# A fused encoder layer on one Trainium2 core: a deeper buffer ring in its first expert stage, a thinner spread of gate batches, and more expert visits in the sample's front

## The reference

```python
h = rmsnorm(x, norm1_g)
na_q, na_k, na_v, r_q, r_k, r_v, r_g = split(h @ w_in)
na_o = neighbourhood_attention(na_q, na_k, na_v, na_rpb)     # 8 heads of 64
ret_o = bidirectional_retention(r_q, r_k, r_v, r_g, ...)     # 4 heads of 128
x = x + concat([na_o, ret_o]) @ w_out
h = rmsnorm(x, norm2_g)
q = h @ w_q                                   # 8 heads, two halves of 128
s = einsum('thpd,hpnd->thpn', q, sub_keys)    # 128 keys for each half
# per head: top 16 of each half, top 16 of the 256 sums -> 16 experts and gates
a = gelu(einsum('td,tkd->tk', h, u[experts]))
x = x + einsum('tk,tkd->td', gates * a, v[experts])
y = rmsnorm(x, final_g)
```

## Time and profile before

| what | value |
|---|---|
| median of 3 runs | 2820.98 us (2814.81 to 2833.08) |
| profiled execution, its own time | 2804.88 us |
| its span | 2803.1 us |
| PE busy | 2431.6 us (87%) |
| DVE busy | 1768.2 us (63%) |
| POOL busy | 1256.0 us (45%) |
| ACT busy | 951.8 us (34%) |
| DMA | 613.60 MB, mean 219 GB/s |

### The profile page before, as it was taken

One profiled execution on the slowest core, in us unless ns is written; L12 is line 12 of the kernel. 1 busy time (PEld: TensorE's weight loads), 2 busy tenths in 40 slices (PEclk: granted clock), 3 DMA queues, 4 the chain that ended last, 5 costly groups with the idle time before them and its releaser, 6 DMA issues.

```text
span 2803.1 us, 34174 instructions
## 1 busy us (share of the span) xinstructions
PE 2431.6 (87%) x12633; PEld 2013.2 (72%) x12633; DVE 1768.2 (63%) x3403; ACT 951.8 (34%) x1426; POOL 1256.0 (45%) x932
## 2 busy tenths in 40 slices
PE   7969788788897898899999987978899798989897
PEld 6759777778875566688888776757677677777775
DVE  5564861132156668659885768768566577777776
ACT  4344344544322322333333322323222233333333
POOL 0001676423453342564444346473677465555530
PEclk9979999999998899899999999999999999999998
DMA  5424556546664443563444477695999899999994
GB/s 188 136 98 145 181 177 208 178 159 188 211 213 134 134 162 137 183 243 119 144 147 145 137 267 277 219 325 164 362 317 326 289 328 325 324 323 324 326 323 173
DMA packets 269189, 613.60 MB, mean 219 GB/s; under 512 B 35920, under 2 KB 134736, under 8 KB 268384
## 3 DMA queue, kind: packets, MB, share of 16 engines
q1 hardware_dynamic: 199008, 402.46, 42.5%
q0 software_dynamic: 67712, 201.61, 21.0%
q10 hardware_dynamic: 2304, 7.34, 0.7%
HBM read 529.51 MB, written 81.79 MB: 218 GB/s over the span
## 4 chain that ended last, share of the span: by engine, by line
PE 47%; DVE 18%; DMA 10%; POOL 9%; ACT 8%; issue 6%; SPq 2%; DVEq 0%; ACTq 0%
PE ps L784 35%; PE ps L814 9%; DMA raw<-in_experts 6%; POOL sp_lo L453 5%; DVE hot_a L1439 3%; DVE acc L1472 3%; ACT sp_hi L671 2%; DVE acc_odd L1472 2%; ACT v_hi L687 2%; DVE hot_b L1435 2%; POOL picked L457 2%; DMA picked<-in_experts,vidx 2%; POOL a_got L462 2%; DMA band<-in_band 1%; SPq L349 1%
## 5 line engine op out<-in xcount | busy, mean ns | idle before, releaser
L784 PE MATMUL ps<-ht_hi,sp_hi 128*128 128x256 f32 (+1 forms) x2048 | 719.0, 351 | 131.7 <-POOL sp_lo L453 73.8
L457 POOL DMA_INDIRECT picked<-in_experts,vidx x384 | 435.8, 1135 | 671.6 <-DVE acc L1472 363.0
L784 PE MATMUL ps<-ht_lo,sp_hi 128*128 128x256 f32 (+1 forms) x2048 | 697.1, 340 | 0.0
L784 PE MATMUL ps<-ht_hi,sp_lo 128*128 128x256 f32 (+1 forms) x2048 | 696.6, 340 | 0.0
L453 POOL TENSOR_TENSOR sp_lo<-raw,sp_hi 128x1024 fp32r<-128x1024 f32 x152 | 384.0, 2528 | 685.0 <-ACT sp_hi L671 685.0
L784 PEld LDWEIGHTS ps<-ht_hi,sp_hi 128*128 128x128 f32 x2048 | 394.8, 193 | 196.0 <-POOL sp_lo L453 91.9
L462 POOL DMA_INDIRECT a_got<-acts,aidx x384 | 432.9, 1127 | 118.4 <-issue 116.2
L784 PEld LDWEIGHTS ps<-ht_hi,sp_lo 128*128 128x128 f32 x2048 | 394.7, 193 | 42.2
L784 PEld LDWEIGHTS ps<-ht_lo,sp_hi 128*128 128x128 f32 x2048 | 395.4, 193 | 36.3
L784 PE MATMUL ps<-v_hi,w_hi 128*128 128x512 f32 x768 | 307.7, 401 | 64.7 <-DVE w_lo L1499 52.4
L679 ACT ACTIVATE act_g<-ps 128x256 f32<-128x256 f32 (+1 forms) x256 | 125.8, 491 | 657.5 <-PE ps L784 653.3
(11 more groups left out here) (180 smaller groups left out, 3440.0 us busy)
## 6 DMA issues: line engine op xcount, KB each, us to landing
raw<-in_experts SPq DMA_DIRECT2D x256, 512.0 KB, 3.6
v_raw<-in_experts SPq DMA_DIRECT2D x128, 512.0 KB, 5.0
raw<-in_front SPq DMA_DIRECT2D x104, 512.0 KB, 3.5
acts<-act_g SPq DMA_DIRECT2D x128, 256.0 KB, 3.3
gates<-stage SPq DMA_DIRECT2D x24, 1024.0 KB, 12.3
act_in<-acts SPq DMA_DIRECT2D x128, 192.0 KB, 5.1
g_in<-gates SPq DMA_DIRECT2D x128, 192.0 KB, 5.3
acts<-act_g SPq DMA_DIRECT2D x128, 128.0 KB, 3.5
```

Of the source, the lines that this page charges most:

```text
L457: pool.indirect_dma_start(picked[n % SLOTS][:, :], None, v_rows, bass.IndirectOffsetOnAxis(ap=vidx[:, n // P, n % P:n % P + 1], axis=0)).t ...
L784: last = pe.matmul(out, l, r, start=start and k == 0, stop=stop and k == 2, skip_group_check=True)
```

## The change

It has five parts.

- **Ring.** In the first u stage all four slots are used: `u_slot` is `step % RING`, each slot has its own semaphore (`u_landed`), loads and `sp_hi` run four steps ahead. POOL splits steps 0 to 55, DVE all of 56 to 127. The sample's first chunks are loaded in steps 124 to 127 and not in step 56, and their split follows the u stage. `EXP_AT` of tile 1 moves from step 42 to 46.
- **Gate batches.** Two to a row, over 16 rows for each tile, from 184, 209 and 234. PE does half of a row's matmuls after each batch. DVE builds them one step ahead, and splits row `step + 1` first. Visits are dealt out by weight, 11 to a step whose next row has gates, 8 to another.
- **Last tile on chip.** Tile 5's gates stay in `stage`; only 256 columns of gates are read back a row, and `w_f` becomes two multiplications, 128 columns from `stage` and 256 from `g_in`. For this `act_in`, `g_in`, `w_f`, `w_hi`, `w_lo`, `x2d`, `fgain`, `junk2` and `acc2` move; several lie where `ht_hi` was, so their first writes wait for the last scores (`a_done` = 256).
- **Visits.** 118 and not 93 in the sample's front: two and not one after each of 10 + 8 + 7 chunks. 138 are left for stage 4.
- **Slots of the front's chunks.** `slot_of` is `c % RING` for both sequences, and the first two loads of the second u stage wait for the last two chunks' split.

```diff
-GATES_AT = {SPARSE: 184, SPARSE + 1: 200, SPARSE + 2: 216}
-GATE_ROWS = 4
+GATES_AT = {SPARSE: 184, SPARSE + 1: 209, SPARSE + 2: 234}
+GATE_ROWS = 16
 TURN_AT = {SPARSE: 161, SPARSE + 1: 171, SPARSE + 2: 179}
-EXP_AT = {0: 25, 1: 42, 2: 140, 3: 152, 4: 164, 5: 174}
+EXP_AT = {0: 25, 1: 46, 2: 140, 3: 152, 4: 164, 5: 174}
...
-FRONT_VISITS = 93
+FRONT_VISITS = 118
...
         acc = [sb("acc0", V0, [P, D_MODEL]), sb("acc1", V0 + 4 * KB, [P, D_MODEL]),
-               sb("acc2", R0 + 28 * KB, [P, D_MODEL])]
+               sb("acc2", A0 + 24 * KB, [P, D_MODEL])]
...
-        act_in = sb("act_in", R0, [P, 2, HALF])
-        g_in = sb("g_in", R0 + 3 * KB, [P, 2, HALF])
-        w_f = sb("w_f", R0 + 6 * KB, [P, 2, HALF])
-        w_hi = sb("w_hi", R0 + 9 * KB, [P, 2, HALF], F32R)
-        w_lo = sb("w_lo", R0 + 12 * KB, [P, 2, HALF], F32R)
-        x2d = sb("x2d", R0 + 16 * KB, [P, SPARSE, D_MODEL])
-        fgain = sb("fgain", R0 + 32 * KB, [P, D_MODEL])
...
+        act_in = sb("act_in", A0 + 21 * KB, [P, 2, HALF])
+        g_in = sb("g_in", A0 + 52 * KB, [P, 2, 2 * P])
+        w_f = sb("w_f", 16 * KB, [P, 2, HALF])
+        w_hi = sb("w_hi", 19 * KB, [P, 2, HALF], F32R)
+        w_lo = sb("w_lo", 22 * KB, [P, 2, HALF], F32R)
+        x2d = sb("x2d", 25 * KB, [P, SPARSE, D_MODEL])
...
         def slot_of(q, c):
-            return (c + 2 * q) % RING
+            return c % RING
...
         for step in range(STEPS):
-            if step < 64 or step < N_KEYS and step % 2 == 0 or N_KEYS <= step < N_KEYS + 56:
+            if step < 56 or N_KEYS <= step < N_KEYS + 56:
                 by_pool[step] = len(by_pool) + 1
             else:
                 by_dve[step] = len(by_dve) + 1
...
-            return step % 2 + 2 * (step // N_KEYS)
+            return step % RING if step < N_KEYS else 2 + step % 2
+
+        def u_landed(step):
+
+            if step < N_KEYS:
+                return u_in[step % RING], 16 * (step // RING + 1)
+            return u_in[step % 2], 16 * (N_KEYS // RING + (step - N_KEYS) // 2 + 1)
...
             def load_chunk(q, c):
                 if c >= RING:
                     sp.wait_ge(*counted(q, "lo_ready", c - RING + 1))
-                elif q and c < 2:
-                    sp.wait_ge(*counted(0, "lo_ready", C_END))
                 elif q:
                     sp.wait_ge(*u_split(N_KEYS - 4 + c))
                 sp.dma_start(raw[:, slot_of(q, c), :], a["front"][c]).then_inc(S[raw_in[slot_of(q, c)]], 16)
...
-                for t in DENSE:
+                for t in DENSE[:-1]:
                     part = step - GATES_AT[t] - GATE_ROWS
                     if 0 <= part < PARTS:
                         sp.wait_ge(S["gate_evac"], 32 * (t - SPARSE + 1))
@@ -368,17 +374,19 @@
...
             def load_weights(r):
                 sp.dma_start(act_in[:, r % 2, :], acts_rows[1][r, :, P:]).then_inc(act_in_done[r % 2], 16)
-                sp.dma_start(g_in[:, r % 2, :], a["gates"][r, :, half_cols(1)]).then_inc(gate_in[r % 2], 16)
+                sp.dma_start(g_in[:, r % 2, :], a["gates"][r, :, SPARSE * P:(NT - 1) * P]).then_inc(gate_in[r % 2], 16)
...
-            for step in range(2):
+            for step in range(RING):
                 sp.wait_ge(*counted(0, "lo_ready", C_END - RING + step + 1))
                 load_u(step)
             for step in range(N_KEYS):
-                sp.wait_ge(*u_split(step))
-                if step + 2 < N_KEYS:
-                    load_u(step + 2)
+                if step + RING < N_KEYS:
+                    sp.wait_ge(*u_split(step))
+                    load_u(step + RING)
+                else:
+                    load_chunk(1, step + RING - N_KEYS)
                 if step:
                     store_act(step - 1)
...
                     load_x(1)
-                    load_chunk(1, 0)
-                    load_chunk(1, 1)
             store_act(N_KEYS - 1)
-            front_loads(1, 2)
+            front_loads(1, RING)
             for step in range(N_KEYS, N_KEYS + 2):
-                sp.wait_ge(*counted(1, "lo_ready", C_END - RING + step - N_KEYS + 1))
+                sp.wait_ge(*counted(1, "lo_ready", C_END - 2 + step - N_KEYS + 1))
                 load_u(step)
...
-            for t in DENSE:
+            for t in DENSE[:-1]:
                 sp.wait_ge(S[f"gate_out{t}"], 16 * PARTS)
...
             for r in range(N_KEYS):
                 if r == 0:
+                    sp.wait_ge(S["a_done"], STEPS)
                     sp.dma_start(x2d[:, :, :], a["x2_park"][:, SPARSE:, :]).then_inc(S["x2_in"], 16)
...
-                elif q and c >= 2:
+                elif q:
                     act.wait_ge(S["a_done"], N_KEYS - 3 + c)
...
-            for step in range(2):
+            for step in range(RING):
                 u_hi(step)
             scores_out(0)
             for step in range(N_KEYS):
                 exponents(step)
                 gelu(step)
-                if step + 2 < N_KEYS:
-                    u_hi(step + 2)
+                if step + RING < N_KEYS:
+                    u_hi(step + RING)
+                elif step + RING - N_KEYS < AHEAD:
+                    hi(1, step + RING - N_KEYS)
...
-                for c in range(2):
-                    if step == NORM_AT + 40 + 5 * c:
-                        hi(1, c)
-            hi(1, 2)
             front(1)
...
-                    for g in range(8):
+                    for g in range(2):
                         gates(t, first + g)
-                        scores(step, g, g + 1)
+                        scores(step, 4 * g, 4 * g + 4)
                 else:
                     scores(step)
...
                 for c in range(C_RET_QK):
                     lo(q, c + AHEAD)
-                    visits(q * (c > 1))
+                    visits(2 * q * (c > 1))
...
-                    visits(q)
...
+                    visits(2 * q)
...
-                        visits(q)
+                        visits(2 * q)
...
                 dve.wait_ge(act_in_done[r % 2], 16 * (r // 2 + 1))
                 dve.wait_ge(gate_in[r % 2], 16 * (r // 2 + 1))
+                if r == 0:
+                    dve.wait_ge(S["a_done"], STEPS)
+                    dve.wait_ge(S["gate_evac"], 32 * SPARSE)
                 if r >= 2:
                     dve.wait_ge(S["w_lo_ready"], r - 1)
-                dve.tensor_tensor(w_f[:, r % 2], act_in[:, r % 2], g_in[:, r % 2], ALU.mult).then_inc(S["w_ready"], 1)
+                dve.tensor_tensor(w_f[:, r % 2, 2 * P:], act_in[:, r % 2, 2 * P:], stage[:, r, :], ALU.mult)
+                dve.tensor_tensor(w_f[:, r % 2, 0:2 * P], act_in[:, r % 2, 0:2 * P], g_in[:, r % 2], ALU.mult
+                                  ).then_inc(S["w_ready"], 1)
...
-                for c in range(2):
-                    if step == NORM_AT + 42 + 5 * c:
-                        lo(1, c)
-            lo(1, 2)
+            for c in range(AHEAD):
+                lo(1, c)
...
+            hot(SPARSE, 0)
+            hot(SPARSE, 1)
+            u_parts(N_KEYS + 56)
             first_free = N_KEYS + 56
+            weight = [11 if gate_window(step + 1) else 8 for step in range(first_free, STEPS)]
             rest = 2 * P - done
             for step in range(first_free, STEPS):
-                window = gate_window(step)
-                share = rest * (step + 1 - first_free) // (STEPS - first_free) - (done - FRONT_VISITS)
+                window = gate_window(step + 1)
+                share = rest * sum(weight[:step + 1 - first_free]) // sum(weight) - (done - FRONT_VISITS)
                 if window:
                     t, first = window
-                    for g in range(8):
-                        hot(t, first + g)
-                        if g == 3:
-                            u_parts(step + 1)
-                        if g % 4 == 1 and share > 0:
-                            visits(1)
-                            share -= 1
+                    u_parts(step + 1)
+                    hot(t, first)
+                    visits(min(share, 1))
+                    hot(t, first + 1)
+                    visits(max(share - 1, 0))
                 else:
-                    u_parts(step + 2)
+                    u_parts(step + 1)
                     visits(max(share, 0))
```

15 lines of the change are left out of this document (9 added, 6 removed).

## The result

The changed kernel takes **2696.6 us** (median of 4 executions, 2686.35 to 2706.84) against 2827.0 (2814.81 to 2833.95): ratio **0.9544**, 95% interval 0.9511 to 0.9578. That is faster, 130 us less, where I had forecast 2655, 166 under the median it was then compared with; the time lies within my range and 42 us above my point.

What follows compares the result with a forecast made beforehand. Latency was taken to bound the first u stage, DVE the twelve gate rows. Terms -89 + 14 - 79 - 8 + 5 = -157 from 2804.88 gave 2648, raised about half way to the median: 2655 us, range 2605 to 2720.

Steps and rivals of the forecast that it cites:

- Part 1: First u stage: with four slots it falls from 485 to 396 us; -89 us, ends -102 and -45.
- the allowance of 13: First u stage: 13 us over PE's 383 for slow POOL split episodes, the norm and loading x.
- Rivals 2 and 3: First u stage: POOL's splits average 3.7 us, 2695 us, chance 0.08; or the ring does not deepen, 2744 us, chance 0.03.
- Part 2: Sample's front: extra visits at POOL's gather pace start attention 11 us later, plus small delays; +14 us, ends +4 and +25.
- Part 3: Steps 184 to 255: 602 us falls to 523.5, DVE bounding gate rows; -79 us, ends -115 and -36.
- 0.33 us a visit: Gate rows, steps 184 to 255: DVE's wait for each gather, making rows 7.65 us, 18 us over PE in 48 rows.
- Rival 4: Gate rows: visits starve, each waiting 2.5 us for its gather; 48 rows lose 239 us, total 2876; chance 0.02.
- Rival 1: Steps 184 to 255: the queue of stores keeps its price, 9.7 us a storing step, total 2698; chance 0.14.
- A second step: Steps 184 to 255: one-hot sets built a step ahead, so a window's first row no longer waits; no separate size.
- Part 4: Seam before the v stage: PE's wait falls from 11.32 to 3.3 us; -8 us, ends -10 and 0.
- Part 5: v stage: the second multiplication adds a start, 64 x 0.07 us; +5 us, bounds 0 and 20.
- the spacing of starts (0.07): v stage: start-to-start times of DVE multiplications price the second piece at 0.07 us, 5 us in all against the page's 10.

Runs made afterwards that it cites:

- e1: The kernel before with the ring's lines only; gates, visits and last tile's store as before: 2753.7 us, ratio 0.9692 to before.
- e9: The changed kernel with DVE's `turned_lo` three steps later in its queue in the first u stage: 2671.3 us, ratio 0.9443 to before.
- e7: The kernel before, unedited, profiled a second time: 2829.68 us in the profiled execution.
- e4: The changed kernel with the last tile's gates stored and loaded again, and one product for the weights: 2700.5 us, ratio 0.9543 to before.
- e6: The changed kernel with one instead of four of DVE's `hot_a` products in each gate batch: 2672.6 us, ratio 0.9398 to before.
- e8: The changed kernel with even visit weights, 8 to 8 instead of 11 to 8, in steps 184 to 255: 2679.2 us, ratio 0.9448 to before.
- e2: The changed kernel with 93 visits in the front again, 163 left for steps 184 to 255: 2742.5 us, ratio 0.9668 to before.
- e5: The changed kernel with front visits at 93, 27 in steps 138 to 183, five in early v rows, weights 11 to 10: 2655.0 us, ratio 0.9343.
- e10: e5 with e9's edit, later POOL fetches, one split moved ahead, and x2d loaded at v row 9: 2625.9 us, ratio 0.9284 to before.
- e11: e10 with the five early v-stage visits put back into steps 184 to 255: 2630.0 us, ratio 0.9272 to before.
- e12: e11 with the loads of x2d and fgain back at row 0 of the v stage: 2621.9 us, ratio 0.9290 to before.
- e3: The changed kernel without the fetch of activations for tiles 0 and 1, visits weighted by the gate alone: 2638.6 us, ratio 0.9325 to before.

## Why the prediction was right, and where it was wrong

The direction, the mechanism of the ring and the order of the terms were right. The sum was 27 us too good.

- **Part 1, the ring, -89:** 82 to 85 measured, and e1 shows it alone. Two sizes were off and cancelled: PE's row is 2.9 us and not 2.99 (the piece I divided was one of projections, not of u rows), and the allowance of 13 should have been near 30, of which 24 were the norm's `turned_lo` (e9). Rivals 2 and 3 did not come: the splits average 2.77 us, and the loop did deepen.
- **Part 2, visits in the front, +14: this is a step that failed.** The front lost 29 against e7 (42 against the first profile; 27 by the means of all versions). I had POOL's pace right, but counted only the last row's landing. The first attention scores came 85 to 94 us after the last gelu in five runs with the extra visits (after, e4, e6, e8, e9) and 67 to 76 in eight without (before, e7, e1, e2, e5, e10, e11, e12): 18 us on the mean, not 11. Left out was the wait for the second group of eight activations (7.75 us; waits for activations 11.4 in all, against 3.8 in e7). In e6, whose front is that of the changed kernel, PE has none of the waits that the trace puts down to nothing, and the scores come at 85.4, 14 over the mean of the eight: so much comes with POOL's pace alone. Left out as well was that PE itself could stop being full, with its clock falling to 0.50, as in 720 to 752 us; the runs leave the cause of that open. In e3, without the activation fetches, the scores come at 67.2.
- **Part 3, steps 184 to 255, -79:** -74 against e7, -62 against the first profile, from which the sum was made. The storing rows came out at 7.01 us against 7.06 forecast. The gate rows failed: 7.98 against 7.65, which is (7.98 - 7.65) x 48 = 16 us. The step was to spread the waits evenly over the rows, 0.33 us a visit, with DVE as the first new bound. The size was nearly right, but 39 rows have PE's pace, and the waits stand in a few rows, as POOL falls behind with its issues. Rival 4 had the place (the split and the sets stand behind the visit that waits), with a small part of its price: DVE's waits for rows are (32.6 + 17.9)/138 = 0.37 us a visit, against 2.5 there, but they come bunched, and e2 shows how near the point was: 25 visits more, and gate rows take 9.22. Rival 1 is refuted by the storing rows. A second step failed with it: the first row of a window was to wait no longer for its sets, and in steps 209, 234 and 235 u is late behind the stores, 11 us in all.
- **Part 4, the seam, -8:** PE's gap is 4.83 against 11.32 in the first profile: -6.5, but -3.7 against the 8.50 of e7. DVE waited 3.81 us for the load of gates, a wait that the sum did not have; its products came behind that.
- **Part 5, the v stage, +5:** from first to last `w_lo` 602.4 us against 596.3 and 597.9: +5 to +6. Of the versions with one product, e4 has 597.3 and e1 600.4, so the term is known to some 2 us only. The two products take 0.63 us from the first's start to the second's end (2076.48 to 2077.11), against 0.55 for one: 0.08 more, which bears out the spacing of starts (0.07). The 0.157 us that the Trainium skill's "VectorE: DVE Perf Modes", section "The TRN2 errata", gives for the length of a second instruction would have made 10 us, twice what was measured.
- **Against the medians:** I went from the first execution only part of the way to the median; every timed execution of the kernel before lies at 2814 or above. That is 15 of the 42 us: 2827 less the forecast's 157 is 2670.

## What to carry to other kernels

Count the issues of every DMA queue that an engine has to feed itself, at the duration that they have beside the work they will stand beside, not at the bare one; here two issues a visit, 2.5 us bare with their spacing, are 4.0 in the gate rows. Work that waits for such fetches belongs where that engine and the one that adds are idle and the bound engine is not touched, even if that is another stage. A deeper ring helps only as far as no engine's list stops in front of a wait that the ring's steps could pass. And a mean wait for each visit says little where a row has slack for it: ask whether the waits come bunched.

## What the hardware showed that I had not expected

Over the traces of the changed kernel, e3, e6 and e10 there are 2816 of POOL's fetches. 514 ran beside no DVE instruction: 0.94 us on the mean. 1475 took over 1.0 us, and 1466 of these end 0.82 us (within 0.04) after the end of a DVE instruction. At four other distances from 0.62 to 1.27 us at most 357 of them do. In 1326 cases that instruction was already running when the fetch began. It can be seen in the rows above: the fetch of 2008.33 ends at 2011.98, and DVE's `hot_b` at 2011.16; the fetch of 2012.29 ends at 2014.89, and the next `hot_b` at 2014.06.

So what matters is less how much DVE work lies beside an issue than whether an instruction of DVE is running when it begins. 372 fetches ran beside nothing but one split of u, v or a chunk. 16 of them found the split running; they took 1.1 to 2.0 us and end 0.81 to 0.82 us after the split. The other 356, all but a few of which began before the split (0.49 us on the mean), took 0.95. Visits do the same: 50 fetches that found nothing but one `acc_odd` running, for 0.33 us on the mean, took 1.74. Among the 1466 the instruction in front was 347 times a visit, 370 times a split, 358 times `w_lo` and 228 times `hot_b`, all of them instructions with two inputs in SBUF. 67 fetches ran beside the softmax's scores, whose input is PSUM, and their maximum, over 0.91 us: 0.94 us. A fetch of 128 x 4 bytes is held up as one of 512 KB is (1.61 and 1.45 us in the last steps).

The Trainium skill, "SBUF — State Buffer", section "SBUF: two separate sides", has this in its warning on a DVE that blocks DMA: while DVE holds the port pair which it shares with GpSimd, GpSimd cannot write the descriptors of its DMAs, and the transfer only seems slow. The trace agrees on the effect; the page's warning names instructions in a 2-port mode, and here visits and plain splits, scalar_tensor_tensor and tensor_tensor with two SBUF inputs, did it too (1.74 us behind a running visit, up to 2.00 behind a running split, against 0.94 bare).
